# The third norm by tokens, one more slot in the expert ring, and h added in PSUM, in a two-block fp32 kernel

## The chip, the cores and the metric

One Trainium2 chip, one NeuronCore. The metric is the time of one execution on the device in microseconds: 1294.65 us, the median of 3 runs (1294.38 to 1295.21). All data is float32. Where precision allows, matrix products run on "rounded" fp32 halves (`F32R`): a number is split into a high part and a low part, and a product is three cheap passes (hi·hi, hi·lo, lo·hi). Plain fp32 products take two instructions each on TensorE.

## The reference

Two transformer blocks with one batch of 256 tokens and width 1024. What matters here, cut from the reference:

```
def first_block(...):                       # gated recurrence + differential attention, then a gated FFN
    ...
    h = h + g2 * ff
    return rmsnorm(h, final_norm_w)         # "final norm" of block 1

def second_block(x, ...):
    h = x
    mix = _hybrid_mixer(_rmsnorm(h, norm_mix_w), ...)   # a second rmsnorm, straight after the first
    h = h + mix
    ffn = _hierarchical_moe(_rmsnorm(h, norm_ffn_w), ...)
    h = h + ffn
    return _rmsnorm(h, norm_final_w)

def rmsnorm(x, w):
    return x * rsqrt(mean(x * x, axis=-1) + EPS) * w
```

So the mixer's input is a norm of a norm ("double norm", here the third norm). With s = sum of h², and s' = sum of (h·w1)², both are scaled copies of h: the first by 1/sqrt(s/D + eps), the double one by 1/sqrt((eps·s + s')/D + eps²). The expert layer picks for each token one of 4 groups and 2 of its 8 experts, 32 experts in all, each with three weight matrices: gate and up (1024 x 512) and down (512 x 1024). All 32 experts' weights are read, 6 MiB each, 192 MiB in total.

## The kernel before

Five engines run programs of their own, in order, and meet at semaphores. Activations lie with features on the partitions and the 256 tokens along the row (`hT`: 8 chunks of 128 features). T is 256, TT = 2 halves of 128 tokens, KC = 8 chunks.

**Matrix products.** All products with shared weights are entries of a list `G`, cut into units of 1024 columns. ScalarE (`split_to`, L1001) writes each unit's high half, VectorE (L1437) its low half, into a ring of three (`WHL`); TensorE (`gemm`, L554) multiplies. A unit can be split only when the unit three before it is multiplied. SyncE loads the weights in 1 MiB pieces. `weave` interleaves the product loops with side work ("lanes") on each engine in an order that is fixed when the program is written; an engine that waits in a lane holds up what is behind it.

**The third norm.** While the last product of the first block (`dn2_1`) is running out, ScalarE squares `hT` chunk by chunk (`third_squares`, L1073) into `scratch`, and VectorE squares it weighed by w1² (`weighed_squares`, L1649) into `sq2`. TensorE (`third_sums`, L691) multiplies a matrix of ones with both, 2 x 8 products of 256 columns, which leaves each sum in all 128 partitions; it then runs 16 idle products (`spin`, L475: an identity times itself into a bank that nobody reads). ScalarE copies one sum to `r1` (L1307), VectorE forms eps·s + s' in `rstd` (L1936), ScalarE takes the root (L1310), VectorE the reciprocal (L1464) and then, for each chunk, hT·w·rstd (L1942); ScalarE and VectorE split it into `XH` (L1067) and `XL` (L1457), and TensorE starts the second block's first product `gd`.

**The final norm of block 1** is wanted only much later, for the residual. ScalarE's lane `final_norm` (L1216) takes the root of `r1`, VectorE's (L1739, L1743) the reciprocal and the eight products, among the products `rv`, `gg` and the retention lanes (L727 sums squares for a group norm, L1210 takes its root).

**Router.** After the last shared product TensorE turns h (`turn_half`, L895), forms the logits (L908), runs 14 idle products, ranks the choices (L925, L926), and runs 15 idle products. VectorE meanwhile finds the experts (L2008 to L2061) and writes `direct` and then `pick` (L2064, L2068), a 0/1 matrix from tokens to slots. Each expert has 64 slots; experts go in pairs (`NPAIR` = 16), and pairs in groups of two. `choose(g)` (L742) collects the tokens of a group by multiplying with `pick`, first the high rows, then the low rows (L2029); `slot_norms` (L770) does the same for the norm factors; `chosen` (L1241 on ScalarE, L1815 on VectorE) copies the result to `xg`.

**Experts.** For each pair TensorE runs gate, up (L943, both with the weights streaming as 512 columns, the two experts side by side in 64 columns of the array each) and down (L981), and `combine` (L792, L794) adds the result for the tokens in banks 0 to 3 over all pairs, starting from zero. ScalarE and VectorE apply the gate (L1393, L2145), copy turned picks and weights (L1399, L1403) and scale the output (L1411, L2156).

**The ring of expert loads.** SyncE (L2335) issues 12 loads of 1 MiB per pair, in the order gate, up, down, in two halves of the chunks and two experts each. They go to 20 slots (`moe_ring`): 2 extra ones, 9 in the arena, the 6 of the shared weights, 2 late ones and `hT`. Load x waits for the release of load x - 20, given by the product that read it (`moe_released`). The first 20 wait for whatever held the slot's memory before. The last down half of the last pair is loaded one chunk at a time (512 KiB, L2333 and L2340).

**The end.** VectorE adds h (`xtok2`) to the four banks (`added`, L2163), ScalarE squares and sums the rows (L1419), VectorE adds the two halves (L2167), root (L1423), reciprocal (L2180), and VectorE multiplies by it and the weights (L2173); SyncE stores four pieces (L2346).

## Time and profile before

| | |
|---|---|
| median of 3 runs | 1294.65 us (1294.38 to 1295.21) |
| the profiled execution | 1297.85 us, span 1296.0 us |
| TensorE matmul | 1252.2 us busy, 97% |
| VectorE, ScalarE | 599.9 us (46%), 490.0 us (38%) |
| moved by DMA | 349.37 MB, mean 270 GB/s |
| chain that ended last | PE 77%, DMA 8%, DVE 6%, SP's queue 4%, ACT 3% |

In the profile PE is TensorE's matmul, PEld its weight load, DVE is VectorE, ACT ScalarE, POOL GpSimd, SP SyncE (SPq: its queue issuing a DMA). The numbers in rows of the timeline are start and length in us from the start of the span, then engine, line, operation, what it writes and reads, and in brackets how long the engine had been idle and who released it. An instruction that waits for several things is shown behind the last of them.

### The profile page before, as it was taken

The numbers are of one execution on the slowest core, as the hardware profiler recorded it, in microseconds if no ns is written. First come the engines' busy times: TensorE is split into PE (matmuls) and PEld (weight loads), VectorE is DVE, ScalarE is ACT, GpSimd is POOL, SyncE is SP. The second block draws the span as 40 slices with busy tenths as digits, with TensorE's granted clock in tenths as the row PEclk, the third lists the DMA queues.
The fourth block names the chain that finished last, engine by engine and source line by source line (L and its number), as shares of the span: only waits on it lengthen the run. The fifth ranks groups of instructions, "written<-read, shape, count | busy, mean of one in ns | idle before, by whom it ended". The sixth has DMA issues, their size and how long they took to land.

```text
span 1296.0 us, 19148 instructions
## 1 busy us (share of the span) xinstructions
PE 1252.2 (97%) x8282; PEld 950.9 (73%) x8282; DVE 599.9 (46%) x963; ACT 490.0 (38%) x744; POOL 78.3 (6%) x83
## 2 busy tenths in 40 slices
PE   8999999999999999999999999999999999999995
PEld 7887888999999989989999999834434344343432
DVE  3575756444546588385765656532122121212112
ACT  4544455434444644465654454521111111111112
POOL 4021000000000122011121000000000000000000
PEclk9999999999999999999999999999999999999998
DMA  9877435655544434355356559889999999999995
GB/s 352 291 262 258 163 103 209 222 182 184 175 147 163 142 131 155 132 187 163 125 164 196 191 164 376 337 359 419 421 420 421 420 421 420 422 420 421 420 420 204
DMA packets 103030, 349.37 MB, mean 270 GB/s; under 512 B 6258, under 2 KB 9760, under 8 KB 78624
## 3 DMA queue, kind: packets, MB, share of 16 engines
q1 hardware_dynamic: 101200, 345.56, 70.3%
q0 software_dynamic: 1568, 2.50, 0.7%
q8 instruction: 66, 1.08, 0.3%
q14 instruction: 20, 0.16, 0.0%
q10 hardware_dynamic: 176, 0.07, 0.0%
HBM read 347.05 MB, written 1.05 MB: 269 GB/s over the span
## 4 chain that ended last, share of the span: by engine, by line
PE 77%; DMA 8%; DVE 6%; SPq 4%; ACT 3%; issue 1%; DVEq 0%; ACTq 0%
PE bank L554 44%; PE bank L943 11%; PE bank L981 6%; SPq L2335 4%; PE bank L742 2%; PE bank L475 2%; DMA arena<-in_expert_w_gate 2%; DMA arena<-in_expert_w_up 2%; DMA hT<-in_expert_w_up 2%; DMA weights<-in_expert_w_up 2%; DVE WHL L1437 2%; PE bank L581 2%; PE bank L511 1%; PE bank L792 1%; PE bank L521 1%
## 5 line engine op out<-in xcount | busy, mean ns | idle before, releaser
L554 PE MATMUL bank<-XH,WHL 128*128 128x256 f32 x2928 | 539.7, 285 | 8.3 <-DVE WHL L1437 4.4
L554 PEld LDWEIGHTS bank<-XH,WHL 128*128 128x128 f32 x2928 | 461.4, 193 | 13.1 <-DVE WHL L1437 6.6
L554 PE MATMUL bank<-XL,WHL 128*128 128x256 f32 x1464 | 414.8, 283 | 0.0
L1437 DVE TENSOR_TENSOR WHL<-weights,WHL 128x1024 fp32r<-128x1024 f32 x223 | 283.0, 1285 | 211.2 <-ACT WHL L1001 210.8
L1001 ACT ACTIVATE WHL<-weights 128x1024 fp32r<-128x1024 f32 x223 | 232.0, 1055 | 208.0 <-PE bank L554 202.7
L554 PEld LDWEIGHTS bank<-XL,WHL 128*128 128x128 f32 x1464 | 282.0, 193 | 0.1
L943 PE MATMUL bank<-arena 128*64 128x512 f32 x480 | 122.3, 595 | 2.7 <-DMA arena<-in_expert_w_up 1.4
L554 PE MATMUL bank<-WHL,XH 128*128 128x512 f32 x320 | 102.1, 394 | 2.6 <-DVE WHL L1437 2.5
L943 PEld LDWEIGHTS bank<-arena 128*64 128x64 f32 x480 | 37.3, 137 | 73.5 <-issue 67.1
L2156 DVE SCALAR_TENSOR_TENSOR y_lo<-bank,small,y_hi 128x512 fp32r<-128x512 f32 x32 | 23.9, 751 | 128.9 <-ACT y_hi L1411 128.2
L554 PEld LDWEIGHTS bank<-WHL,XH 128*128 128x128 f32 x320 | 60.1, 188 | 17.4 <-DVE WHL L1437 4.1
L943 PE MATMUL bank<-weights,arena 128*64 128x512 f32 x288 | 68.3, 595 | 3.4 <-DMA weights<-in_expert_w_gate 2.1
L1411 ACT ACTIVATE y_hi<-bank,small 128x512 fp32r<-128x512 f32 x32 | 21.9, 687 | 113.2 <-PE bank L981 111.7
L2145 DVE SCALAR_TENSOR_TENSOR chainm<-bank,small,chainm 128x512 f32<-128x512 f32 x16 | 12.0, 752 | 109.0 <-PE bank L943 109.0
L554 PE MATMUL bank<-WHL,XL 128*128 128x512 f32 x160 | 62.4, 390 | 0.0
L1403 ACT ACTIVATE masks<-bank 128x512 f32<-128x512 f32 x16 | 9.6, 598 | 132.4 <-PE bank L964 132.4
L981 PE MATMUL bank<-arena,masks 128*64 128x512 f32 x232 | 57.6, 596 | 1.4 <-ACT masks L1403 1.4
L943 PEld LDWEIGHTS bank<-weights,arena 128*64 128x64 f32 x288 | 21.7, 137 | 46.1 <-issue 37.4
L1393 ACT ACTIVATE chainm<-bank,small 128x512 f32<-128x512 f32 x16 | 11.0, 687 | 105.9 <-PE bank L943 105.9
L981 PEld LDWEIGHTS bank<-arena,masks 128*64 128x64 f32 x232 | 17.4, 137 | 35.5 <-issue 32.3
L943 PE MATMUL bank<-late_weights,arena 128*64 128x512 f32 x96 | 41.1, 595 | 0.8 <-DMA late_weights<-in_expert_w_gate 0.8
L475 PE MATMUL bank<-ident 128*128 128x128 f32 x296 | 40.0, 299 | 0.3 <-DVE arena L2008 0.3
(361 smaller groups left out, 1337.2 us busy)
## 6 DMA issues: line engine op xcount, KB each, us to landing
weights<-in_w_in SPq DMA_DIRECT2D x58, 1024.0 KB, 5.0
arena<-in_expert_w_up SPq DMA_DIRECT2D x31, 1024.0 KB, 26.1
arena<-in_expert_w_gate SPq DMA_DIRECT2D x29, 1024.0 KB, 26.2
arena<-in_expert_w_down SPq DMA_DIRECT2D x29, 1024.0 KB, 26.5
weights<-in_w_ada SPq DMA_DIRECT2D x22, 1024.0 KB, 7.5
weights<-in_expert_w_down SPq DMA_DIRECT2D x18, 1024.0 KB, 26.2
weights<-in_expert_w_gate SPq DMA_DIRECT2D x18, 1024.0 KB, 25.9
weights<-in_expert_w_up SPq DMA_DIRECT2D x18, 1024.0 KB, 26.2
```

The lines of the kernel that those rows point to most:

```text
L475: e.matmul(bank[b][:, 0:P], ident[:, :], ident[:, :], start=True, stop=True)
L511: ins = e.matmul(bank[b][32 * q:32 * q + 32, :], c32[:, 4 * r + q, :], in_slot(f"ada{ADA[i]}", r, 4, 512)[:, q, :], start=r == 0, stop=r == 1)
L554: ins = e.matmul(o, l, r, start=first, skip_group_check=True, stop=g.part == g.parts - 1 and k == g.kc - 1 and n == 2)
L581: ins = e.matmul(bank[b][:, h * P:(h + 1) * P], K[:, h, si * P:(si + 1) * P], Q[:, h, ti * P:(ti + 1) * P], start=True, stop=True)
L742: ins = e.matmul(bank[banks[q]][:, kk * T:(kk + 1) * T], u[:, j, k * P:(k + 1) * P], pick[:, j, :], start=u is uhi and kk == 0 and j == 0, ...
L943: ins = e.matmul(bank[b][64 * s_:64 * s_ + 64, :], xg[:, k, p % 2 * P + 64 * s_:p % 2 * P + 64 * s_ + 64], moe_weights(x, 4, HID)[:, kk, : ...
L981: ins = e.matmul(bank[6 + n][64 * s_:64 * s_ + 64, :], hpT[:, k, 64 * s_:64 * s_ + 64], moe_weights(x, 2, D)[:, 0 if alone else kk, n * 51 ...
L1001: e.activation(unit_halves(U)[0], unit_weights(g, u), ACT.Copy).then_inc(S.w_hi, 1)
L1411: e.activation(yo[n][0], bank[6 + n][:, :], ACT.Copy, scale=slot_weight[:, p % 2:p % 2 + 1]).then_inc(S.m_ya, 1)
L1437: e.tensor_tensor(lo, unit_weights(g, u), hi, ALU.subtract).then_inc(S.w_lo, 1)
L2156: e.scalar_tensor_tensor(out=yo[n][1], in0=bank[6 + n][:, :], scalar=slot_weight[:, p % 2:p % 2 + 1], in1=yo[n][0], op0=ALU.mult, op1=ALU. ...
L2335: e.dma_start(moe_weights(x, kc // 2, HID if wi < 2 else D), src[:, half * kc // 2:(half + 1) * kc // 2, :]).then_inc(moe_landed(x)[0], 16)
```

## The change

- Third norm: the squares are multiplied as the stationary operand, token half by token half, with a two-column moving operand: w1² and ones (`wmix` gets a third row of ones). Both sums come out per token (2 columns per half) in one bank. Copy, product, roots and reciprocals work on 128x2 (`token_fin`, `token_rstd`). `third_spread` on TensorE spreads both reciprocals over the partitions (a column broadcast times the identity, 2 products each); VectorE reads the double norm's from bank 5, ScalarE copies the other to `r1`. `weighed_squares`, `sq2` and ScalarE's lane `final_norm` go; VectorE's keeps only its eight products. The idle products behind go from 16 to 5.
- Router: the 14 idle products behind the logits are replaced by four products identity x `xtok2` into banks 0 to 3 (`start=True`), and `combine` adds to them. At the end ScalarE's squares and VectorE's last products read the banks; `added` goes. (A branch that runs only when an expert has over 64 tokens copies the banks back first.)
- Picks of group 0: `direct` and `pick` are written by token half, and `choose(0)` waits for each half of its own; its `slot_norms` move behind the gate product of pair 0. ScalarE's copy of them comes behind its two exponentials, and VectorE's picks of group 1 wait for them.
- Ring: a 21st slot, the first 2048 columns of the arena, where `xtok2` was; free when the places are copied (`S.posc`).
- Pieces: `moe_pieces` lists them. In the last pair the second half of up is loaded in two pieces of 512 KiB per expert; the last down half stays as it was.

```
     def third_sums(ks):
         for k in ks:
-            for i, x in enumerate((scratch, sq2)):
-                ...
-                ins = e.matmul(bank[4 + i][:, 0:T], ones[:, :], x[:, k, :], start=k == 0, stop=k == KC - 1, ...)
+            w.wait_ge(S.sq, KC + k + 1)
+            for j in range(TT):
+                ins = e.matmul(bank[4][:, 2 * j:2 * j + 2], scratch[:, k, j * P:(j + 1) * P], wmix[:, 1:3, k],
+                               start=k == 0 and j == 0, stop=k == KC - 1 and j == TT - 1, ...)
...
+    def third_spread():
+        clear(5)
+        w.wait_ge(S.rstd, 2)
+        spread(bank[5][:, 0:T], token_rstd).then_inc(S.across, 1)
+        free[5] = (S.u2, KC)
+        clear(4)
+        w.wait_ge(S.fin_v, 1)
+        spread(bank[4][:, 0:T], token_fin).then_inc(S.across, 1)
+        free[4] = (S.r1, 1)
...
     third_sums(range(4, KC))
-    spin(7, 16)
+    third_spread()
+    spin(7, 5)
...
     logits(1)
-    spin(7, 14)
+    for i in range(4):
+        j, n = divmod(i, 2)
+        clear(i)
+        e.matmul(bank[i][:, :], ident[:, :], xtok2[:, j, n * 512:(n + 1) * 512], start=True, stop=False, ...)
...
     # choose(0)
+    for j in range(TT):
+        w.wait_ge(S.m_slots, j + 1)
         for q in range(4):
             clear(banks[q])
-            rows_of(uhi, q)
+            rows_of(uhi, q, [j])
...
-    if g == 0:
-        slot_norms(0, 3)
...
     # experts, behind the gate product
+    if wi == 0 and p == 0:
+        slot_norms(0, 6)
...
     # ScalarE, third norm
-    w.wait_ge(S.ss, 2)
-    e.activation(r1[:, :], bank[4][:, 0:T], ACT.Copy).then_inc(S.r1, 1)
-    w.wait_ge(S.rs2, 1)
-    e.activation(rstd[:, :], rstd[:, :], ACT.Sqrt, bias=eps2[:, 0:1], scale=1.0 / D).then_inc(S.rms, 1)
+    w.wait_ge(S.rs2, 2)
+    e.activation(token_rstd, token_rstd, ACT.Sqrt, bias=eps2[:, 0:1], scale=1.0 / D).then_inc(S.rms, 1)
+    e.activation(token_fin, token_fin, ACT.Sqrt, bias=epsc[:, 0:1], scale=1.0 / D).then_inc(S.fin_a, 1)
     for k in range(KC):
         split_x(46 + k, k, scratch[:, k, :], (S.u2, k + 1))
+    w.wait_ge(S.across, 2)
+    e.activation(r1[:, :], bank[4][:, 0:T], ACT.Copy).then_inc(S.r1, 1)
...
     # VectorE, third norm
-    weighed_squares(range(4, KC))
-    w.wait_ge(S.r1, 1)
-    e.scalar_tensor_tensor(out=rstd[:, :], in0=r1[:, :], scalar=EPS, in1=bank[5][:, 0:T], ...)
-    norm_rstd(1)
+    w.wait_ge(S.ss, 2)
+    e.tensor_copy(token_fin, bank[4][:, 1:2 * TT:2]).then_inc(S.rs2, 1)
+    w.wait_ge(S.rs2, 1)
+    e.scalar_tensor_tensor(out=token_rstd, in0=token_fin, scalar=EPS, in1=bank[4][:, 0:2 * TT:2], ...)
+    w.wait_ge(S.rms, 2)
+    e.reciprocal(token_rstd, token_rstd).then_inc(S.rstd, 1)
+    w.wait_ge(S.fin_a, 1)
+    e.reciprocal(token_fin, token_fin).then_inc(S.fin_v, 1)
+    w.wait_ge(S.across, 1)
     for k in range(KC + 2):
         if k < KC:
             e.scalar_tensor_tensor(out=scratch[:, k, :], in0=hT[:, k, :], scalar=wmix[:, 0, k:k + 1],
-                                   in1=rstd[:, :], ...).then_inc(S.u2, 1)
+                                   in1=bank[5][:, 0:T], ...).then_inc(S.u2, 1)
...
     # VectorE, picks
     if p % 2 == 0 and p + 2 < NPAIR:
         w.wait_ge(S.m_ch, 4 * (p // 2 + 1))
+        w.wait_ge(S.m_r, p // 2 + 1)
...
     # the end, ScalarE and VectorE
-    w.wait_ge(S.acc, i + 1)
-    e.activation((hp, maskf[:, 0:HID])[n], xtok2[:, j, n * 512:(n + 1) * 512], ACT.Square, ...)
+    w.wait_ge(S.m_cb, 4 * (NPAIR - 1) + i + 1)
+    e.activation((hp, maskf[:, 0:HID])[n], bank[i][:, :], ACT.Square, ...)
-    e.scalar_tensor_tensor(out=normed[:, j, c0:c1], in0=xtok2[:, j, c0:c1], ...)
+    e.scalar_tensor_tensor(out=normed[:, j, c0:c1], in0=bank[2 * j + n][:, c0 - 512 * n:c1 - 512 * n], ...)
...
+    moe_ring += [(arena[:, 0:SLOT], sem("row_slot_loaded"), (S.posc, 1), None)]
...
+    def moe_pieces(p):
+        if p == NPAIR - 1:
+            return [(0, 0, 4), (0, 4, 4), (1, 0, 4), (1, 4, 2), (1, 6, 2), (2, 0, 2), (2, 2, 1), (2, 3, 1)]
+        return [(0, 0, 4), (0, 4, 4), (1, 0, 4), (1, 4, 4), (2, 0, 2), (2, 2, 2)]
```

## Rows read from the trace of the kernel before

**Rows 1.** Busy time by windows (start:end, length, busy per engine, granted clock, DMA share, GB/s).

```profile
784.00:836.00 52.00, 49.31 (x325) 44.42 (x325) 32.42 (x65) 26.58 (x37) 0.00 (x0) 1.00 1.01 419
...
838.00:846.00 8.00, 8.00 (x56) 5.42 (x56) 5.72 (x20) 4.55 (x9) 0.00 (x0) 1.00 0.00 1
...
848.00:1272.00 424.00, 412.29 (x1971) 172.26 (x1968) 83.12 (x211) 60.84 (x130) 0.00 (x0) 1.00 1.01 421
```

**Rows 2.** Timeline of SyncE's queue (start, length), around 836.

```profile
828.59 0.33 SPq L2335 DMA_DIRECT2D hT<-in_expert_w_up  x1
845.72 0.81 SPq L2335 DMA_DIRECT2D extra_weights<-in_expert_w_down  x2
```

**Rows 3.** Timeline, router and first gate product.

```profile
833.90 3.60 PE L475 MATMUL bank<-ident 128*128 128x128 f32 x30
...
834.52 0.26 ACT L1378 ACTIVATE arena<-bank 128x64 f32<-128x64 f32 x1
...
836.46 0.69 DVE L2068 TENSOR_TENSOR picks<-chainm 128x512 fp32r<-128x512 f32 x1
...
841.16 0.95 PE L770 MATMUL bank<-arena,picks 128*128 128x1 f32 x8
842.04 3.65 PE L943 MATMUL bank<-extra_weights,arena 128*64 128x512 f32 x16
```

**Rows 4.** Timeline, third norm; last the instructions of line 1942 (min/median/max ns).

```profile
408.25 7.14 PE L691 MATMUL bank<-arena,ones 128*128 128x256 f32 x32 [0.25 <-ACT arena L1073]
...
409.55 1.59 ACT L1073 ACTIVATE arena<-hT 128x256 f32<-128x256 f32 x4 [0.53 <-DVE hT L1624]
...
416.85 1.75 DVE L1464 RECIPROCAL spare<-spare 128x256 f32<-128x256 f32 x1 [0.57 <-ACT spare L1310]
...
420.35 0.36 PE L554 MATMUL bank<-XH,WHL 128*128 128x256 f32 x1 [1.38 <-issue]
...
L1942 DVE SCALAR_TENSOR_TENSOR arena<-hT,wmix,spare x8: 479/480/486, 418.6 to 423.1; 128x256 f32<-128x256 f32 x8
```

**Rows 5.** Timeline, norm of heads in the first block; last the instructions of line 1609.

```profile
175.73 0.20 DVE L1553 RECIPROCAL small<-small 128x8 f32<-128x8 f32 x1 [4.58 <-ACT small L1120]
175.99 2.05 PE L499 MATMUL bank<-ident,small 128*128 128x128 f32 x16 [0.55 <-DVE small L1553]
...
L1609 DVE SCALAR_TENSOR_TENSOR arena<-arena,pcol,bank x4: 475/476/479, 177.2 to 182.5; 128x256 f32<-128x256 f32 x4
```

**Rows 6.** Busy time by windows, third norm and the start of gd.

```profile
408.00:421.00 13.00, 11.31 (x68) 10.14 (x67) 8.81 (x20) 5.04 (x14) 0.00 (x0) 1.00 0.10 36
...
422.00:423.00 1.00, 1.00 (x5) 0.99 (x6) 1.00 (x4) 0.55 (x2) 0.00 (x0) 0.50 0.00 0
```

**Rows 7.** Timeline, around the final norm of block 1.

```profile
615.60 1.75 DVE L1739 RECIPROCAL spare<-spare 128x256 f32<-128x256 f32 x1 [4.24 <-ACT spare L1216]
...
617.61 0.59 PE L727 MATMUL bank<-arena,ones 128*128 128x256 f32 x2
619.46 0.39 PE L554 MATMUL bank<-XH,WHL 128*128 128x256 f32 x1 [1.26 <-DVE WHL L1437]
```

**Rows 8.** The end: chain that ended last, then windows, then timeline.

```profile
1220.40 7.02 PE bank L981 x32
...
1264.79 7.89 PE bank L943 x32
...
1274.96 6.28 PE bank L981 x28
...
1276.00:1278.00 2.00, 2.00 (x12) 0.58 (x10) 0.00 (x0) 0.00 (x0) 0.00 (x0) 1.00 0.58 233
1278.00:1279.00 1.00, 1.00 (x8) 0.42 (x6) 0.00 (x0) 0.00 (x0) 0.00 (x0) 1.00 0.08 33
...
1283.68 2.02 DVE L2163 TENSOR_TENSOR arena<-bank,arena 128x512 f32<-128x512 f32 x3
1284.40 0.63 ACT L1419 ACTIVATE chainm<-arena 128x512 f32<-128x512 f32 x1 [1.60 <-DVE arena L2163]
```

More of the change, by code:

```diff
@@ L249, in build @@
         theta = small[:, 88:89]
+        token_rstd, token_fin = small[:, 90:92], small[:, 92:94]
         assert b4.at <= ARENA - KC * T
@@ L417, in build @@
         X_SQUARES, X_RMS, X_RSTD, X_BOUNDS, X_LAMBDA = 2, 3, 4, 5, 6
-        S.sqrt_table, S.sq, S.sqw, S.ss, S.rms, S.rstd, S.nrm = (sem("norm_" + n) for n in (
-            "table", "squares", "weighed_squares", "sums", "rms", "rstd", "scaled"))
+        S.sqrt_table, S.sq, S.across, S.ss, S.rms, S.rstd, S.nrm = (sem("norm_" + n) for n in (
+            "table", "squares", "spread", "sums", "rms", "rstd", "scaled"))
         S.scl, S.lb_v, S.lam_v, S.lam_p, S.chain = (sem(n) for n in (
@@ L2172, in times_row @@
                     if c0 // 512 == n:
-                        ins = e.scalar_tensor_tensor(out=normed[:, j, c0:c1], in0=xtok2[:, j, c0:c1],
+                        ins = e.scalar_tensor_tensor(out=normed[:, j, c0:c1],
+                                                     in0=bank[2 * j + n][:, c0 - 512 * n:c1 - 512 * n],
                                                      scalar=small[:, 34 + j:35 + j], in1=f_, op0=ALU.mult, op1=ALU.mult)
@@ L2337, in sync @@
-            for s_ in range(2):
-                x = 12 * NPAIR + s_
-                w.wait_ge(*moe_released(x - len(moe_ring)))
-                e.dma_start(moe_weights(x, 2, D)[:, 0, :],
-                            a["expert_w_down_2"][0, NE - 2 + s_].rearrange("(p k) n -> p k n", p=P)[:, 3, :]).then_inc(
+                for wi, k0, kn in moe_pieces(p):
+                    for s_ in range(2):
+                        x, _ = moe_load(p, wi, k0, s_)
+                        name = ("gate", "up", "down")[wi]
+                        src = a[f"expert_w_{name}_2"][0, 2 * p + s_].rearrange("(p k) n -> p k n", p=P)
+                        if x >= len(moe_ring):
+                            w.wait_ge(*moe_released(x - len(moe_ring)))
+                        elif moe_ring[x][2] is not None:
+                            w.wait_ge(*moe_ring[x][2])
+                        else:
+                            w.wait_ge(*free[moe_ring[x][3]])
+                        if wi == 2 and kn == 1:
+                            e.dma_start(moe_weights(x, 2, D)[:, 0, :], src[:, k0, :]).then_inc(moe_landed(x)[0], 16)
+                        elif wi == 2:
+                            e.dma_start(moe_weights(x, 2, D), src[:, k0:k0 + 2, :]).then_inc(moe_landed(x)[0], 16)
+                        else:
+                            e.dma_start(moe_weights(x, 4, HID)[:, 0:kn, :], src[:, k0:k0 + kn, :]).then_inc(
```

126 lines of the change are left out of this document (45 added, 81 removed).

## The prediction

> **What bounds the kernel now.** I read the busy time by windows first, with the DMA share as its last columns. From 784 to 836 us the core takes in 419 GB/s, from 838 to 846 nothing, and from 848 to 1272 again 421 GB/s [rows 1]. The last two fifths of the kernel are thus one stream of expert weights with one hole in it. The queue's own timeline says what makes the hole: the twentieth load, into hT, is issued at 828.59, and the next only at 845.72 [rows 2], since the ring has 20 slots and slot 0 is given back by the first half of the first gate product. That product starts at 842.04 [rows 3]. So the end is (the moment of the first release) + (loads not yet made) at 421 GB/s + a tail. Two things move it one for one: an earlier first release, and a load that falls into the hole. TensorE's busy share of 97% (412.29 of 424 us even in the stream) misleads here: shorter TensorE work inside the stream would be worth nothing, except at its very end.
>
> Ahead of the stream TensorE is the chain itself, and time is won only where it waits or does work that it needn't. I looked for those places with the timeline around each edited line: 408 to 420 (the third norm, [rows 4]), 613 to 619 (the final norm's reciprocal, [rows 7]), and 841 (the slot norms, [rows 3]). Last comes the tail behind the stream [rows 8].
>
> **The third norm, by tokens.** Before: 32 instructions of 256 columns, 408.25 to 415.39 [rows 4], then copy, product, square root and a reciprocal over 256 columns of 1.75 us that ends at 418.60; the first normed chunk starts in the next 0.03 us, at 418.63, and TensorE gets its halves at 420.35, 1.72 us later. After: again 32 instructions (8 chunks, 2 token halves, 2 passes each), but 2 columns wide. The nearest row is 8 instructions of width 1 in 0.95 us [rows 3], 0.119 each, so 3.81 us: the sums end at 412.06. The squares don't hold them up: the last ends by 411.14 [rows 4], and the eighth chunk is reached at 408.25 + 28 x 0.119 = 411.58. The chain behind: a copy and a product of 2 columns (I take 0.17 each, a little under the 0.20 of an 8-column reciprocal, [rows 5]), a root (0.27, a little over the 0.26 of ScalarE's 64-column copy, [rows 3]), the reciprocal 0.20, four hand-overs of 0.04, then the spread over partitions. For that the first block has the same pattern: a reciprocal ends at 175.93 and the product that reads the spread bank starts at 177.19, 1.26 us for 8 of the 16 instructions [rows 5]; with 4 it is 1.26 - 4 x 0.119 = 0.78. Together 1.75 us, so the first normed chunk starts at 413.81 in place of 418.63: **4.8 us**. The second spread (0.48) and five idle products (10 instructions at 3.60/30 = 0.12, 1.2 us, [rows 3]) end near 415.3, and the first chunk's halves come at 413.81 + 1.72 = 415.5, so they stay just hidden. The weighed squares that go from VectorE, and the late copy of r1 (ScalarE, behind the eight splits) are beside the path: the next weights' half that the copy pushes back by 0.4 us is used over 1 us later. If that cover is gone, it costs 0.4.
>
> What this could cost is the clock. Before, TensorE idled for 1.38 us up to 420.35 [rows 4], and from 422 the granted clock was 0.50, 1.2 GHz [rows 6]. The new sums are narrower and a 1.0 us idle stretch comes right behind. At 1.2 GHz the later half of the sums, both spreads and the five idle products take twice as long: about 1.0 + 0.5 + 1.0 = 2.5 us. The other side: if the drop falls earlier, the gd product no longer runs in it, +0.5. Bounds 2.3 to 5.3; I take 4.8, since the mean from 408 to 421 was 1.00 [rows 6] and the drop came only after a longer gap.
>
> The new products read the scale from PSUM. Here the rows show 475/476/479 ns with a bank operand (line 1609) and 479/480/486 without (line 1942), both 128x256 [rows 4, 5]. The Trainium skill (VectorE: DVE Perf Modes, "The TRN2 errata") speaks against the change: it gives 120 cycles of fixed cost for a PSUM source and 58 for an SBUF one. By it the eight products would cost 62/0.96 = 65 ns more each, 0.5 us in all, and this term would be an estimated 4.3. The trace disagrees, and the sum keeps 4.8.
>
> **The final norm.** The reciprocal over 256 columns on VectorE (615.60, 1.75 us, [rows 7]) and the root with its table load on ScalarE just ahead of it go; two-column ones at 413 replace them. Now they hold up the next weights' halves, and TensorE stands idle from the end of the two instructions at 617.61 to 619.46, 1.26 us by the row [rows 7]; at a pitch of 0.21 those two end nearer 618.04, so 1.42. With both gone the low half, ready only 1.2 us after the two products of hT that follow the reciprocal, comes 1.75 us and the root's share earlier, before TensorE needs it. The table load that the next root then needs falls into ScalarE's wait for the fold. I take **1.35 us** (bounds 0 and 1.42).
>
> **Router and picks.** Four fp32 products of 128x512 take the place of 14 idle ones (28 instructions at 0.12, 3.4 us). The 32 instructions of a down product, which run in pairs of column halves, take 7.02 us [rows 8], 0.44 for one pair, and a seed is two passes, 0.88: so 3.5 us, and TensorE then waits for the selection as before: **0**. Picks by token half: both halves together end at 836.46 + 0.69 = 837.15, the first half alone would be there at about 836.3, but the 15 idle products in front of choose(0) run from 833.90 until about 837.3 [rows 3] and stay. So **0**; VectorE pays two more short waits, which the low rows, needed 2 us into choose(0), absorb. The slot norms leave the path ahead of the first gate product: 0.95 us [rows 3]. The first release comes that much earlier, less a little because the gate product now meets xg while it is being copied: **0.9 us** (0 to 1.0). They run again behind the gate product, so the up product starts when it did; that costs nothing, as four slots, 10 us of load, are free by then. VectorE's new wait for them, with the picks of group 1, the weights of pair 0 and its hidden product queued behind, ends at about 841.1 + 6.9 + 0.95 = 849; the picks and weights, some 3 us, are then done before the up product, another 6.9 us, and its transposes.
>
> **One more slot.** Its load waits for the place copy on ScalarE (834.78, [rows 3]) and is issued 1.4 us before the queue runs dry. 1.049 MB at 421 GB/s are 2.49 us, all inside a hole of 8 us and more, even after the hole has shrunk by 0.9. **2.5 us** (0 to 2.5). The seeds that read its memory are long done.
>
> **Smaller last pieces.** The last up product takes 7.89 us for its 32 instructions; undisturbed, 32 take 7.02 [rows 8], so 0.87 us of it is waiting for its second half. In halves of 512 KB the first two chunks are there 2.5 us earlier and the last two when they were, with 1.7 us of products left: the wait goes. **0.8 us**. Down then starts 0.8 earlier, and is TensorE's to the end: its last chunk is reached three quarters of 7.02 us after its start, at 1274.96 - 0.8 + 5.3 = 1279.5, and the loads have ended by 1279 (33 GB/s in the last window, [rows 8]).
>
> **Rows of h in PSUM.** At the end VectorE's three additions (2.02 us, [rows 8]) precede ScalarE's squares. ScalarE can now start where the first addition did, at 1283.68 in place of 1284.40, 0.72 us; the second square moves equally, as do the two of the second token half behind the first root. All later steps hang on the last of these squares. **0.7 us** (0 to 0.75).
>
> **Sum.** 4.8 + 1.35 + 0.9 + 2.5 + 0.8 + 0.7 = 11.05 us. The profiled execution took 1297.85 (span 1296.0, 1.85 around it), so it would take 1286.8. The runs without it have a median of 1294.65, 3.2 less, and I take the difference from there: 1283.6.
>
> **The rivals.**
> - The clock drops while the narrow sums run. For: the drop at 422 [rows 6] shows that this spot is near the edge. Against: a mean of 1.00 up to 421. Price 2.5, time 1286.1. Chance 12%.
> - The extra slot earns nothing, as its load is late or the first release is what counts twice. Against: 1.4 us of margin. Time 1286.1. Chance 6%.
> - Half-size pieces slow the stream's end. For: the last windows move 233 and 33 GB/s. Against: there the queue is running out. If the 2.1 MB of new pieces went at 233 in place of 421, 4.0 us, and the gain of 0.8 were lost, 1288.4. Chance 5%. The Trainium skill (DMA: Bandwidth & Descriptors, "Bandwidth") says to batch DMAs to 1 MiB or more for three quarters of peak, which speaks for this rival; no row here separates it from the drain.
> - The picks by half do bring choose(0) forward, because the idle products are not what it waits for: up to 0.9 more, 1282.7. Chance 6%.
> - Slower than before: an uneven ring of 21 lowers the rate of the whole stream. Its price is 426 us (171 loads of 2.49) times the loss; it eats 11.05 us from a loss of 2.6%, below 410 GB/s, and from 3.2% on, under 408, it is slower by over 0.2%. Against: 419 and 421 GB/s in stretches with quite different waits [rows 1]. At 3.5% 1298.5. Chance 2%.
>
> **The numbers.** The forecast has 69%, its own range 1282.4 to 1285.0. The range for 8 in 10 is 1281.9 to 1286.9: at the low end all upper bounds (11.8) and the picks' 0.9, at the top the 2.5 us rivals with a small loss beside. What a measurement tells from no change is about 0.2%, 2.6 us: faster 0.96 (all cases but the last, with a rest), same 0.02, slower 0.02.
>
> **What would show it.** The sums' 32 instructions span 3.8 us and the first norm product starts 4.8 us earlier, at a clock of 1.00. TensorE has no wait near 617. The first gate product starts about 7.05 us earlier, at 835.0; the hole is 3.4 us shorter, and the stream still moves 421 GB/s. The last up products show no wait, and the squares start directly behind the first combined bank. I am wrong if the hole shrinks by less than 3 us, if the clock falls between 408 and 416, or if the windows of the stream fall under 418 GB/s.

## The result, and the profile after

The changed kernel takes 1281.39 us (median of 6 runs, 1279.94 to 1282.90), the kernel before 1295.10 us in the same session (6 runs, 1294.38 to 1296.92): ratio 0.9891, 95% interval 0.9878 to 0.9905. I had forecast 1283.6, range 1281.9 to 1286.9. The gain, 13.7 us by the medians, is larger than the forecast's 11.05, and the time lies 0.5 us under the range.

Two things of the kernels' own must be taken out before the terms can be compared. Both kernels have two levels: the changed one 1279.95 (three runs) and 1282.85 (three), the one before about 1294.7 (four) and 1296.8 (two). At equal level the gain is 14.7 us at the lower one, 13.9 at the upper. The 1294.65 that the forecast started from belongs to before's lower level. And the profiled execution of before belongs to the upper level, that of the changed kernel to the lower. The busy time by windows shows why (columns as in [rows 1]; the third figure from the right is the granted clock). Before:

```profile
18.00:20.00 2.00, 2.00 (x15) 2.00 (x15) 0.94 (x7) 0.92 (x3) 2.00 (x3) 0.75 1.05 399
20.00:22.00 2.00, 2.00 (x12) 2.00 (x11) 0.00 (x0) 0.00 (x0) 0.26 (x1) 0.50 1.04 387
```

After, the same stretch:

```profile
18.00:20.00 2.00, 2.00 (x19) 1.91 (x18) 0.51 (x5) 0.00 (x0) 1.09 (x2) 1.00 1.05 400
20.00:22.00 2.00, 2.00 (x18) 0.54 (x18) 0.00 (x0) 0.00 (x0) 0.00 (x0) 1.00 1.01 372
```

TensorE worked at 1.2 GHz around 20 us in the one execution and at 2.4 in the other, in code that the change doesn't touch. So I cut the span at starts that both traces have, and compare stage by stage (us; each figure is the difference of two starts in a timeline, the last two end with VectorE's last product and with the span, which is printed to 0.1 us):

| stage | before | after | gain | forecast |
|---|---|---|---|---|
| start to first product of the first gemm | 30.25 | 27.44 | 2.81 | none |
| to the sums of the third norm | 378.00 | 378.04 | 0.0 | 0 |
| to the product behind gd (L869 / L878) | 29.02 | 24.10 | 4.92 | 4.8 |
| to the router's place product | 396.16 | 394.51 | 1.65 | 1.35 |
| to the first gate product | 8.61 | 8.07 | 0.54 | 0.9 |
| to the last down product | 432.92 | 429.64 | 3.28 | 2.5 + 0.8 |
| to the end of VectorE's last product | 15.28 | 14.43 | 0.85 | 0.7 |
| to the end of the span | 5.76 | 2.07 | 3.69 | none |

The terms that I had summed come to 11.24 against 11.05. That this is so near is in part luck, since their errors have both signs: the slot norms gave 0.36 less than I took, the final norm 0.30 and the rows of h 0.15 more. What is over lies at the two ends, where the sum had no term.

**The third norm**, timeline of after (start, length, engine, line, what it writes and reads), which answers to [rows 4]:

```profile
405.48 3.74 PE L691 MATMUL bank<-wmix,arena 128*128 128x2 f32 x32 [0.25 <-ACT arena L1085]
409.25 0.16 DVE L1934 COPY small<-bank 128x2 f32<-128x2 f32 x1 [2.32 <-PE bank L691]
409.44 0.16 DVE L1936 SCALAR_TENSOR_TENSOR small<-small,bank 128x2 f32<-128x2 f32 x1
409.70 0.30 ACT L1315 ACTIVATE small<-small,eps 128x2 f32<-128x2 f32 x1 [2.22 <-DVE small L1936]
410.02 0.17 DVE L1939 RECIPROCAL small<-small 128x2 f32<-128x2 f32 x1 [0.42 <-ACT small L1315]
410.25 2.08 PE L498 MATMUL bank<-ident,small 128*128 128x128 f32 x8 [1.03 <-DVE small L1939]
411.51 1.26 DVE L1945 SCALAR_TENSOR_TENSOR arena<-hT,wmix,bank 128x256 f32<-128x256 f32 x3 [1.13 <-PE bank L498]
412.12 2.34 PE L474 MATMUL bank<-ident 128*128 128x128 f32 x10
414.11 0.56 PE L553 MATMUL bank<-XH,WHL 128*128 128x256 f32 x1
```

And the windows, which answer to [rows 6]:

```profile
408.00:409.00 1.00, 1.00 (x11) 1.00 (x10) 0.00 (x0) 0.00 (x0) 0.00 (x0) 1.00 0.00 0
409.00:415.00 6.00, 4.97 (x24) 4.88 (x24) 4.14 (x14) 2.53 (x8) 0.00 (x0) 0.50 0.00 0
416.00:421.00 5.00, 5.00 (x43) 4.90 (x42) 3.86 (x7) 3.09 (x6) 3.08 (x6) 1.00 0.19 35
```

The sums take 3.74 us for 32 instructions, as worked out; but from 409 the clock is 0.50, so the eight instructions of the two spreads take 2.08 us and the ten idle ones 2.34, not 1.2. VectorE's eight products with a bank operand take 472 to 479 ns each, no more than before [rows 4, 5]. The first of them starts 6.03 us after the sums, 10.38 before: 4.35 us earlier, not the 4.8 that I had named as the sign, and the first product of gd comes 3.47 us earlier (8.63 against 12.10). Only the end of the stage has 4.92.

**Router and first gate product** ([rows 3]):

```profile
824.53 3.59 PE L474 MATMUL bank<-ident 128*128 128x128 f32 x30
826.55 0.42 DVE L2073 TENSOR_TENSOR picks<-chainm 128x256 fp32r<-128x256 f32 x1
827.62 0.42 DVE L2073 TENSOR_TENSOR picks<-chainm 128x256 fp32r<-128x256 f32 x1
827.88 2.15 PE L752 MATMUL bank<-picks,rows_hi 128*128 128x256 f32 x16
829.87 2.08 PE L752 MATMUL bank<-picks,rows_lo 128*128 128x256 f32 x16
831.27 1.57 ACT L1248 ACTIVATE arena<-bank,arena 128x256 f32<-128x256 f32 x4 [5.91 <-PE bank L752]
832.16 0.20 PEld L955 LDWEIGHTS bank<-extra_weights,arena 128*64 128x64 f32 x4 [0.42 <-ACT arena L1248]
```

The first half of the picks is there at 826.97, and the products that use it start at 827.88, when the idle ones are through. The gate's weight load now waits 0.42 us for the copies of the picked rows: that is the part of the slot norms' 0.95 that didn't come back.

**The hole and the stream** ([rows 1, 2]); SyncE's queue, then windows:

```profile
819.21 0.33 SPq L2334 DMA_DIRECT2D hT<-in_expert_w_up  x1
825.39 0.33 SPq L2332 DMA_DIRECT2D arena<-in_expert_w_down  x1
835.84 0.80 SPq L2332 DMA_DIRECT2D extra_weights<-in_expert_w_down  x2
```

```profile
784.00:825.00 41.00, 38.38 (x212) 31.59 (x212) 23.90 (x54) 23.01 (x33) 0.00 (x0) 1.00 1.01 421
840.00:1250.00 410.00, 399.80 (x1927) 167.52 (x1926) 85.29 (x219) 59.73 (x127) 0.00 (x0) 1.00 1.01 421
```

The new load is issued at 825.39, while the loads before it are still moving, and the rate stays 421 GB/s. By the transfers themselves the hole is 9.1 us before (no expert load from 837.6 to 846.7) and 6.2 after (830.6 to 836.8), 2.9 us less.

**The end** ([rows 8]); the chain that ended last:

```profile
1252.47 7.07 PE bank L955 x32
...
1261.80 6.28 PE bank L993 x28
...
1271.26 0.69 ACT masks L1427 x2
...
1275.84 0.39 DVE arena L2174
```

The last up product has lost its wait (7.07 us, before 7.89). From its start to that of the last down product are 9.41 us, before 10.23. Then comes what no row of mine had shown. The transfers between the end of VectorE's last product and the end of the program, before (1290.3 to 1295.9; packets, MB, share):

```profile
q1 hardware_dynamic: 288, 0.52, 25.1%
q8 instruction: 1, 0.02, 1.1%
q14 instruction: 1, 0.01, 0.5%
```

and after (1276.3 to 1278.3):

```profile
q1 hardware_dynamic: 288, 0.52, 70.5%
```

The same output is stored, but before, two packets of instructions come behind it (q8 carries TensorE's: 66 packets of 16 KB in the whole trace of before, 65 after, and 65 or 66 with its records in the runs below), and the program ends 3.7 us later. Whose wait that is, the last instructions of the program say, all of them the jump over the body that only tokens beyond an expert's 64 slots need. On the other engines it takes at most 0.07 us; on TensorE (PEldq is its sequencer; duration in ns three times, then the start) before and after:

```profile
L2503 PEldq COMPARE_BRANCH  x1: 4068/4068/4068, 1291.9 to 1291.9; - x1
L2510 PEldq COMPARE_BRANCH  x1: 369/369/369, 1277.9 to 1277.9; - x1
```

The branch starts 1.7 us behind VectorE's last product in both, and its 4.07 and 0.37 us are the whole difference.

### The profile page after: what moved, and what is told of

Same layout as the page of the kernel before. It is cut to its first block, busy times and chain, and to the rows that moved or that the text cites. A ratio compares the mean times of both kernels' runs of the same rounds, so it can differ in the third digit from the quotient of the medians.

```text
span 1278.3 us, 19076 instructions
## 1 busy us (share of the span) xinstructions
PE 1241.9 (97%) x8248; PEld 942.4 (74%) x8248; DVE 591.8 (46%) x955; ACT 488.7 (38%) x744; POOL 81.5 (6%) x83
## 4 chain that ended last, share of the span: by engine, by line
PE 82%; DMA 6%; DVE 6%; ACT 3%; SPq 1%; issue 1%; DVEq 0%; ACTq 0%
PE bank L553 45%; PE bank L955 14%; PE bank L993 7%; PE bank L752 3%; DMA weights<-in_expert_w_gate 2%; PE bank L474 2%; DMA weights<-in_expert_w_up 2%; DMA arena<-in_expert_w_up 2%; PE bank L580 2%; DVE WHL L1445 2%; PE bank L510 1%; SPq L2334 1%; PE bank L800 1%; PE bank L802 1%; PE bank L520 1%; ACT WHL L1013 1%
## 5 line engine op out<-in xcount | busy, mean ns | idle before, releaser
L955 PE MATMUL bank<-arena 128*64 128x512 f32 x476 | 140.9, 595 | 3.4 <-DMA arena<-in_expert_w_gate 2.1
L955 PEld LDWEIGHTS bank<-arena 128*64 128x64 f32 x476 | 42.7, 137 | 72.9 <-issue 65.1
L955 PE MATMUL bank<-weights,arena 128*64 128x512 f32 x288 | 81.1, 596 | 5.6 <-DMA weights<-in_expert_w_gate 4.2
L993 PE MATMUL bank<-arena,masks 128*64 128x512 f32 x264 | 75.6, 596 | 0.7 <-ACT masks L1411 0.7
L955 PEld LDWEIGHTS bank<-weights,arena 128*64 128x64 f32 x288 | 24.8, 137 | 48.2 <-issue 35.8
L993 PEld LDWEIGHTS bank<-arena,masks 128*64 128x64 f32 x264 | 24.1, 137 | 34.6 <-issue 31.9
L2132 DVE TENSOR_SCALAR picks_turned<-masks 128x256 fp32r<-128x256 f32 x16 | 4.7, 294 | 76.4 <-ACT masks L1407 76.3
L1113 ACT ACTIVATE arena<-arena 128x1024 f32<-128x1024 f32 x16 | 17.0, 1060 | 52.9 <-DVE arena L1516 44.7
```

The source lines that it names most:

```text
L955: ins = e.matmul(bank[b][64 * s_:64 * s_ + 64, :], xg[:, k, p % 2 * P + 64 * s_:p % 2 * P + 64 * s_ + 64], moe_weights(x, 4, HID)[:, kk, : ...
L993: ins = e.matmul(bank[6 + n][64 * s_:64 * s_ + 64, :], hpT[:, k, 64 * s_:64 * s_ + 64], moe_weights(x, 2, D)[:, kk, n * 512:(n + 1) * 512] ...
L1113: e.activation(E, E, ACT.Exp, scale=L.escale).then_inc(L.exp, 1)
```

## The experiments

In each, the edit is made to the changed kernel unless another is named. All were timed beside 7 to 15 runs of the kernel before, whose lowest is 1294.22 to 1294.26 each time and 1294.38 in the first session, so lowest runs can be set against the changed kernel's 1279.95. Differences of single stretches are worth less: where nothing was edited between the first gate product and the last down product, that stretch takes 429.41 to 429.69 us in seven traces. A record is one of TensorE's products, weight loads or sequencer instructions in the profile.

**1. Sixty-eight more TensorE records, hidden.**

```
  for p in range(NPAIR):
+     spin(5, 2 if 5 <= p < 12 else 3 if p == 12 else 0)
      for wi in range(2):
```

> The changed kernel with 17 more idle products (68 records on TensorE, as many as the change had taken away) put ahead of the gates of pairs 5 to 12 of the expert stage, where each pair has over 8 us in which TensorE waits for weights. Theory (code fetch): the 3.7 us by which the program ends sooner behind its last vector instruction (2.07 us against 5.76) are a fetch of TensorE's instructions (the instruction queue q8, 16 KB) when it jumps over the body that isn't taken; whether the target has already been fetched hangs on how many instructions stand before it. Then this kernel is 3 to 3.7 us slower than the changed one, q8 has 66 packets and one of them lies behind the last store, and all starts up to the last vector instruction are unchanged. Rival (the end's own edit: rows of h in PSUM, stores unchanged): no change, 0 us, q8 as in the changed kernel. Rival (the idle products delay the stream): last vector product later by up to 9 us.

Measured: lowest runs 1283.03, 1283.05 against 1279.95, so +3.1 us. VectorE's last product ends at 1276.12 (changed kernel 1276.23), the span at 1281.3. From 1276.2 to 1281.3, and TensorE's last branch:

```profile
q1 hardware_dynamic: 288, 0.52, 27.7%
q8 instruction: 1, 0.02, 1.4%
q14 instruction: 1, 0.01, 0.6%
...
L2511 PEldq COMPARE_BRANCH  x1: 3552/3552/3552, 1277.8 to 1277.8; - x1
```

The fetch is back, with nothing of the end's own edit touched.

**2. The kernel before, moved the other way.**

```
  for p in range(NPAIR):
+     spin(5, 4 if 3 <= p < 13 else 7 if p == 13 else 0)
      for wi in range(2):
```

> The kernel before with 47 more idle products (188 records on TensorE) in pairs 3 to 13 of the expert stage, so that its end stands at the same place within a block of 256 instructions as the end of the changed kernel. Theory (code fetch): the program ends 2.1 us behind the last vector instruction in place of 5.76, so 3 to 3.7 us faster than before (about 1291.3), with no q8 packet between the last store and the end. Rival (the end's own edit): same as before, within 0.2%. Rival (idle products delay the stream): slower.

Measured: 1294.65 us median of 11 runs, lowest 1292.72; before 1296.39 of 15, lowest 1294.22; ratio 0.9990, interval 0.9981 to 0.9999. In its profile the time behind VectorE's last product is 2.12 us in place of 5.76, and from 1289.2 to 1291.2 there is no packet of instructions, and TensorE's branch is short:

```profile
q1 hardware_dynamic: 290, 0.52, 70.5%
...
L2504 PEldq COMPARE_BRANCH  x1: 369/369/369, 1290.8 to 1290.8; - x1
```

The runs gain 1.5 us by the lowest and 1.7 by the medians, not the 3 to 3.7 expected. Part of the rest is in the trace: from the first gate product to the last down are 433.93 us, 432.92 before, of which 0.79 is a longer wait of the last up product (11.02 us from its start to the last down, 10.23 before). What takes the remaining 1 us or so in the runs isn't shown. The tail itself behaves as expected with the old code of the end, so the rival (the end's own edit) is out from both sides.

**3. Ring of 20.**

```
- moe_ring += [(arena[:, 0:SLOT], sem("row_slot_loaded"), (S.posc, 1), None)]
```

> The changed kernel with the extra slot of the ring taken away (20 slots). By the prediction the slot is worth 2.5 us (bounds 0 to 2.5): the load behind it can be issued only when the first gate products have released a slot. Expected: last vector product 2.4 to 2.5 us later than in the changed kernel, end fetch absent as there, time 2.4 us above it. Rival (a further slot earns nothing, the transfers are limited by releases later on): 0 us.

Measured: lowest 1282.36, profiled execution 1282.57 against 1279.97, +2.6; gate to down 432.27 us against 429.64, +2.63. The hole is 8.6 us long, 6.2 with the slot. The slot is worth one load of 2.49 us in the hole.

**4. Ring of 20, and the end as before.** The seeds go (14 idle products stand in their place), the additions return:

```
- e.matmul(bank[i][:, :], ident[:, :], xtok2[:, j, n * 512:(n + 1) * 512], start=True, stop=False, ...)
+ spin(7, 14)
...
+ e.tensor_tensor(o, bank[2 * j + n][:, :], o, ALU.add).then_inc(S.acc, 1)
```

> As ring20, and the rows of h are no longer put into PSUM: seeds of the four banks out (14 idle products again in their place), the four additions on VectorE at the end again. Compare with ring20, whose slot count it shares. By the prediction +0.7 to 0.85 us at the end of the program. The code-fetch theory: the end behind the last vector instruction stays at 2.1 us or goes to 5.8 according to the 40 more TensorE records, and q8's packets tell which. The end's-own-edit theory: the gap of 5.76 us is back whatever q8 shows.

Measured: last down to VectorE's end 15.28 us as before, against 14.43: the edit is worth 0.85. The stretch behind it is 5.18 us, with the packets from 1282.5 to 1287.6:

```profile
q8 instruction: 1, 0.02, 1.4%
q14 instruction: 1, 0.01, 0.6%
```

This kernel has 16,749 TensorE records, the changed one 16,709. The median 1289.36 against ring20's 1282.72 mixes this fetch (3.1), the 0.85 and unequal levels; lowest against lowest it is 4.1, about the sum of the first two (3.95).

**5. Both norms as before** (sums of 256 columns over two sets of squares, root and reciprocal on all columns).

```
- ins = e.matmul(bank[4][:, 2 * j:2 * j + 2], scratch[:, k, j * P:(j + 1) * P], wmix[:, 1:3, k], ...)
+ ins = e.matmul(bank[4 + i][:, 0:T], ones[:, :], x[:, k, :], ...)
```

> The changed kernel with the third norm and the final norm made the old way again (sums of 256 columns for two sets of squares, sq2 on VectorE, square roots and reciprocals of 256 columns on every partition). By the prediction's terms 4.8 + 1.35 us slower; by the milestones of the two traces 4.9 + 1.5 us. TensorE gets 28 records more than the changed kernel (16,737), between 16,709 (no fetch behind the last store) and 16,749 (fetch): with a fetch the whole is 6.2 to 6.4 + 3.1 us, without one 6.2 to 6.4 us; the tail behind the last vector instruction (2.1 or 5.2 us) tells which. The granted clock should be 1.00 from 409 to 416 and fall in the products of gd, as in the kernel before. Rival (the drop of the clock in the narrow sums cost the gain there): less than 4 us between the third sums and the products behind gd.

Measured: 1291.95 median, lowest 1289.78, 9.8 above the changed kernel's (9.3 to 9.5 expected with a fetch); behind VectorE's last product 5.12 us, so with 16,736 records the fetch is there. The third-norm stage takes 28.48 us, 24.10 in the changed kernel; the stretch to the router's place product 396.22, against 394.51. Here the clock did not fall at all in or behind the norm, unlike in [rows 6]:

```profile
408.00:421.00 13.00, 11.52 (x69) 10.33 (x70) 8.81 (x20) 4.86 (x13) 0.00 (x0) 1.00 0.07 27
421.00:423.00 2.00, 1.66 (x10) 1.05 (x9) 2.00 (x7) 1.24 (x3) 0.00 (x0) 1.00 0.00 0
```

So of before's 29.02 us, 0.54 were its fall of the clock in gd (29.02 - 28.48), which the old norm has in some executions and not in others: experiment 2, with the same norm, has it from 420.4 to 423.7 us, and its stage takes 29.36. I had expected it in this trace, and it wasn't there.

**6. Slot norms ahead of the gate again.** They take bank 3, which holds rows of h in this kernel, so a part of the output is lost.

```
+ if g == 0:
+     slot_norms(0, 3)
...
- if wi == 0 and p == 0:
-     slot_norms(0, 6)
```

> The changed kernel with the slot norms of the first group again in front of the first gate product. Prediction's term: 0.9 us later (bounds 0 to 1.0); by the two traces 0.5 us, since the first gate product waits for ScalarE's copies of the picked rows (xg) in any case. Same number of TensorE records, so the tail stays 2.1 us. Rival (nothing, since the copies alone set the start): 0 us.

Measured: place product to gate 8.59 us against 8.07, so 0.52 (8.07 to 8.11 in the other traces with the fifteen idle products, but 8.36 in experiment 1's); lowest run 1280.26, +0.3 us. The gate to the last down is 0.27 shorter (429.37), hardly more than that stretch varies. The 0.9 of the prediction is refuted, the 0.5 of the traces holds at the place.

**7. Last up weights whole.**

```
- return [..., (1, 0, 4), (1, 4, 2), (1, 6, 2), (2, 0, 2), ...]
+ return [..., (1, 0, 4), (1, 4, 4), (2, 0, 2), ...]
```

> The changed kernel with the last up weights of the last pair in whole pieces again, 8 TensorE products wait for 1 MB and not for 0.5 MB. Prediction's term 0.8 us (bounds -4 to 0.87); by the traces 0.84. The stream stays at 421 GB/s in both. Rival (half pieces slow the stream): this kernel is faster.

Measured: gate to down 430.37 us, +0.73; last up to last down 10.07 us against 9.41, +0.66; lowest 1280.58, +0.6. The half pieces pay.

**8. Idle products cut.**

```
+ spin(3, 2)
  ada_turn(0)
- spin(3, 12)
+ spin(3, 3)
...
- spin(7, 5)
+ spin(7, 1)
...
- spin(7, 15)
+ spin(7, 10)
```

> The changed kernel with idle products cut at three places, to see which of them stand on the path: at the start 2 + 3 in place of 12 around the turn of the first ada row (18.8 to 20 us), 1 in place of 5 ahead of gd, 10 in place of 15 ahead of the picks. Theory: the idle products at the start are on the path (2.9 us in the chain), so the first product of the gemms comes 2.2 us earlier; the fall of the granted clock that some executions have at 20 us goes or stays with the two idle products in the 0.95 us gap ahead of the turn. Ahead of gd the first product comes 0.9 us earlier, but the products behind gd don't, because VectorE's splits (0.73 us each, eight of them) end the stage: 0. Ahead of the picks the first half of the picks is there 0.9 us before the products start: 0.4 us or less, since the last products wait for the low rows that VectorE writes until 830.3. Sum 2.2 to 2.7 us faster than the changed kernel. Rival (the clock falls where idle products are missing): no gain at the start or a loss of up to 2 us. Tail 2.1 us (44 TensorE records less).

Measured: 1279.76 median of 4 (1278.35 to 1280.79), the lowest 1.6 us below the changed kernel's, where 2.2 to 2.7 were expected. First product of the gemms at 25.71, 1.73 us earlier (not 2.2: its weights now come last); 0.31 of it is lost again before 404. Ahead of gd the first product is 1.0 us earlier, the stage behind it ends 24.19 us after the sums' start, against 24.10: nothing, as expected. Ahead of the picks 0.36 us.

**9. The sums 128 columns wide.**

```
- ins = e.matmul(bank[4][:, 2 * j:2 * j + 2], ..., wmix[:, 1:3, k],
+ ins = e.matmul(bank[4][:, j * P:(j + 1) * P], ...,
+                wmix[:, 1:3, k].unsqueeze(1).broadcast_to([P, P // 2, 2]),
```

> The changed kernel, where the sums of the third norm write 128 columns (the two useful ones repeated 64 times) instead of 2. The number of TensorE records and their weight loads stay; each of the 32 products took 117 ns with 2 columns, and the idle products of 128 columns take 117 ns too, so the sums should still take 3.7 to 3.8 us. Theory (the granted clock falls to 0.50 at 409 because of products that move only 2 columns): with 128 columns the clock stays 1.00 from 409 to 416, the spread of the sums takes 1.0 to 1.1 us instead of 2.08, VectorE's first norm product comes 0.5 us earlier after the start of the sums (5.56 instead of 6.03), and the stage behind it ends 0.5 us earlier or more, if no later fall takes it back: 0.3 to 1 us faster. Rival (the clock falls because TensorE waits from 409.2 to 410.2 for VectorE and ScalarE): the clock falls as before, 0 us.

Its timeline and its windows:

```profile
405.75 3.82 PE L691 MATMUL bank<-wmix,arena 128*128 128x128 f32 x32 [0.25 <-ACT arena L1086]
410.60 1.16 PE L498 MATMUL bank<-ident,small 128*128 128x128 f32 x8 [1.03 <-DVE small L1940]
411.35 1.26 DVE L1946 SCALAR_TENSOR_TENSOR arena<-hT,wmix,bank 128x256 f32<-128x256 f32 x3 [0.62 <-PE bank L498]
```

```profile
408.00:410.00 2.00, 1.57 (x15) 1.38 (x13) 0.32 (x2) 0.00 (x0) 0.00 (x0) 1.00 0.00 0
410.00:412.00 2.00, 1.40 (x12) 1.40 (x13) 0.98 (x4) 0.61 (x3) 0.00 (x0) 1.00 0.00 0
412.00:414.00 2.00, 1.74 (x13) 1.37 (x13) 2.00 (x7) 1.48 (x4) 0.00 (x0) 1.00 0.00 0
```

Same 32 instructions, same 1.03 us wait behind them, 64 times the columns in 3.82 us instead of 3.74: and the clock stays at 1.00 where it was 0.50. The spreads take 1.16 us for 2.08, the first norm product comes 5.60 us after the start of the sums and not 6.03, and the stage takes 23.68 us and not 24.10: 0.42 us. One trace of each would not rule out chance, but the others agree: in all nine traces with the narrow sums the granted clock goes to 0.50 within 2.8 to 4.8 us of their start and stays there for 6.8 us, and the stage takes 24.10 to 24.73 us (median 24.26); in both with the wide ones (this and experiment 10) it stays at 1.00, and the stage takes 23.68 and 23.66. The mean granted clock of every single execution fits: 0.997 to 0.999 in the eight with the wide sums, 0.994 to 0.997 in the ten of the changed kernel. The narrow products, not the wait, let the clock fall, at a price of 0.4 to 1.0 us in the stage. In the whole time nothing is clear of the noise: 1279.35 to 1281.80, median 1280.95, beside 1280.03 to 1283.00, median 1280.11, of the changed kernel (experiment 12).

**10. Experiments 8 and 9 together.**

> The idle products cut as in idle_cut, and the sums written 128 columns wide: a candidate for the fastest kernel. Expected 1.6 us (idle_cut's gain in its profile) plus 0.3 to 1 us below the changed kernel's 1279.95 in executions of the same clock at the start, so 1277.3 to 1278.3; if the clock falls all the same with one idle product ahead of gd, 1278.3.

Measured: 1278.18 us median of 4 (1277.70 to 1279.56), the fastest kernel; ratio to before 0.9871, interval 0.9853 to 0.9888. Against the changed kernel's own runs on the same chip (1280.03 to 1283.00) the lowest is 2.3 us lower, and it lies in the 1277.3 to 1278.3 expected.

**11. The gap at the start filled.**

```
+ spin(3, 2)
  ada_turn(0)
- spin(3, 12)
+ spin(3, 10)
```

> The changed kernel with two of the twelve idle products of the start moved into the 0.95 us in which TensorE waits for ScalarE ahead of the turn of the first ada row; the same number of instructions. Theory (that gap makes the granted clock fall to 0.50 for 3.4 us at about 20 us in some executions, worth 2.8 us): all executions are at the lower of the two levels, 1279.5 to 1280. Rival (the fall has another cause, it is there or not by chance of when the chip looks): the two levels stay, near 1279.5 and 1282.4.

Measured: 1279.01, 1279.26, 1279.58 and 1281.73. First gemm product at 26.87, 0.57 earlier, as two idle products now run in the wait. By its time one of four is at the upper level still (no profile shows its clock), so the gap is probably not the fall's only cause.

**12. The changed kernel again.**

> The changed kernel itself, on the same chip and beside the same runs of the kernel before, to see how often each of its two levels comes (1279.95 and 1282.85 in its first six executions, three each). Both theories on the start: two levels, 2.9 us apart.

Measured: 1280.03, 1280.09, 1280.14 and 1283.00. The profiled one is the one at the upper level, with the same fall at 20 us that before's profile had:

```profile
18.00:20.00 2.00, 2.00 (x15) 2.00 (x14) 0.94 (x7) 0.86 (x3) 2.00 (x3) 0.73 1.05 400
20.00:22.00 2.00, 2.00 (x11) 2.00 (x11) 0.00 (x0) 0.00 (x0) 0.20 (x1) 0.50 1.04 385
```

One of four here, three of six in the first session, and with experiments 3, 4, 6 and 7, which have the same code at the start, 15 of 29 executions by their times. Four runs, one of them at the upper level, are too few to say whether experiment 11 made the fall rarer. That is left open.

## Why the prediction was wrong, step by step

**The step that failed is the last one of the sum**: "The runs without it have a median of 1294.65, 3.2 less, and I take the difference from there: 1283.6." It carries the terms to the end of the program as if all behind VectorE's last product stayed; that stretch was put at nothing without a reason. At equal level the runs differ by 14.7 us and my terms make 11.05; the rest, 3.65, is this stretch, which went from 5.76 to 2.07 us. (The stages as measured add up to 14.93, 0.2 more than the runs differ.) Experiments 1 and 2 show what it is: at the end TensorE jumps over a body that isn't taken (the work for overflowing experts), and in the kernel before it must then fetch the code behind it, within a branch of 4.07 us that takes 0.37 without a fetch. It fetches none with 16,645 records (experiments 8 and 10), 16,709 and 16,963 (experiment 2), and fetches with 16,736, 16,749, 16,775 and 16,777. The change takes 66 records from TensorE: 40 net by the rows of h (14 idle products out, four products in), 28 net by the third norm (11 idle products out, the spreads in), and 2 sequencer instructions come to it. Undoing either alone brings the fetch back (experiments 4 and 5). It fits that the jump's target moved into code already fetched: a packet of q8 comes about every 250 records, the last one ahead of the end at record 16,568 before and 16,581 after, thus in the same block, and experiment 2, by adding 188, gets the next packet, at record 16,835, ahead of the jump. The three others that fetch (experiments 1, 4 and 5) have branches of 3.49 to 3.55 us and so lose 3.1 us by it, before itself 3.7; in before the packet begins 1.5 us into the branch, in the three 0.95, and why, no run shows.

The page of the profile of before has both numbers that point to it, 66 packets of q8 and 8,282 products with as many weight loads, some 250 TensorE instructions per packet; no sentence of the prediction is about the stretch behind the last store. The Trainium skill knows the mechanism: "Runtime: NRT & Kernel Launch", "Instruction fetch mechanics", says that a taken branch whose target lies outside the fetched pages stalls until the target's page is there, and "Advanced Engine Details and Errata", "ISA Cache", gives 256 instructions to a line of 16 KB. The trace agrees with both (a q8 packet inside the 4.07 us branch; 250 records to a packet of 16 KB) and adds the price, 3.1 us here. With that price, which only the experiments gave, the forecast would have been 1280.5.

What I called 1.85 us around the span and 3.2 us to the median was mostly a level: the fall of the clock at 20 us, 2.8 us, in that one execution. To take the difference from the median was right; to call 1281.4 the result of one distribution isn't, since it is the middle between 1279.95 and 1282.85. The upper of these lies inside my range, the lower 2.0 us under it; like with like, the miss is 3.65 us, more than the 2.2 of the medians.

**Third norm, 4.8.** The stage gave 4.92, but not by the path that I gave. The rival that the clock falls during the narrow sums (12%) is what happened; I had priced it at 2.5 us (by its own rows more: the later half of the sums alone is 1.9 us, not 1.0). It cost 0.42 in this pair of traces, 0.4 to 1.0 in all of them (experiment 9), since the sums were nearly through when it fell and VectorE, which gives a chunk each 0.73 us, ends the stage in any case: idle products at half speed ahead of gd delay nothing that counts. And 0.54 came back, as before's own fall in gd was gone; that was my "+0.5". With neither, 28.48 to 23.68 is 4.80 us, the forecast's value for a clock of 1.00. The number is thus right in part by luck: two falls of the clock that nearly cancel in this pair of traces. One condition under which I had called myself wrong was met, without its price. PSUM as a source costs VectorE nothing here: 474 ns against 480. By the fixed costs in the Trainium skill ("VectorE: DVE Perf Modes", "The TRN2 errata"), 120 cycles for a PSUM source and 58 for an SBUF one, it should have cost an estimated 65 ns more each; the measurement decides against it.

**Final norm, 1.35**: 1.65 between the product behind gd and the router's place product, 1.71 against experiment 5, and 1.45 at the least between any two traces of the two kinds, above my upper bound of 1.42. At the place itself 1.54 are seen (TensorE products of the two traces 7.82 us apart ahead of it, 9.36 behind), more than TensorE's idle time there had been. What else was won isn't shown; that the root with its table load delayed ScalarE's halves beyond this stretch is only a guess.

**Slot norms, 0.9**: 0.54 and 0.52. I had written that the gate product "now meets xg while it is being copied" and took "a little" off; it is 0.42 us, half of the gain.

**Picks by half, 0**: right, and for the reason given, the idle products. Cutting five of them gives 0.36 (experiment 8), not 0.9, probably because the low rows are late next: the products with them then take 2.35 us for 2.08.

**Extra slot, 2.5**: 2.45 by the stage, 2.63 by experiment 3. **Smaller pieces, 0.8**: 0.82 by the stage, 0.66 to 0.73 by experiment 7. **Rows of h in PSUM, 0.7**: 0.85 twice, 0.1 over my upper bound. The first square comes 0.72 us earlier, as I had it; the rest is in ScalarE's four squares, which take 0.63, 0.63, 0.61 and 0.61 us from SBUF before and 0.60, 0.60, 0.58 and 0.59 from the banks after. The rivals of the slot, of small pieces and of a slower stream are out: 421 GB/s in all windows.

The hole shrank by 2.9 us (0.54 + 2.45 = 3.0 by the stages), not by 3.4, and so just met another condition under which I had called myself wrong. Most of what it lacks is the slot norms' term. What made the forecast miss was elsewhere.

## What to carry to other kernels

Read the trace behind the last store too. Here the span ended 2.1 us after the last vector instruction, or 5.2 to 5.8; see then whether an instruction queue has a packet there and how long each engine's last branch is. With a jump over a rarely taken body at the end, adding or removing some idle products where they are hidden can move it, here 3.7 us of the 14.7 that the change seemed to bring. Before terms are added to a median, find out which level of the clock the profiled execution and each run were at. And where narrow products are bound by their weight loads, try them wider: here 64 times the columns cost 0.08 us for 32 instructions and kept the clock.

## What the hardware showed that I had not expected

- An instruction of 2 columns takes 117 ns (3.74 us / 32) and one of 128 columns 119 ns (3.82 / 32), but only the wide ones keep the granted clock at 1.00; behind 3.7 us of the narrow ones it was 0.50 from 409 to 415.8, and so in nine traces of nine, against none of two with the wide ones.
- TensorE's own code fetch in a jump at the end costs 3.1 us (a branch of 3.55 us against 0.37), and comes and goes with 27 records more or less (16,709 and 16,736).
- At the start the clock falls to 0.50 for about 3.4 us in some executions and not in others, with the same code: 2.8 us on the whole kernel (its first gemm product at 30.25 or 27.44 us).
